# A hybrid diffusion trunk step on one core: the order of VectorE, ScalarE and TensorE around five waits of the trunk

## The reference, cut to what matters

```
h = rms_norm(x) * (1 + sc1) + sh1                    # sh1, sc1, ... = silu(cond) @ w_ada + b_ada
u2, q, k, v, f, g = split(h @ w_in)
conv = silu(layer_norm(depthwise_conv31(glu(u2)))) @ w_conv_out
attn = attention(q, k, v) @ w_na_out
fnet = fft2(f).real @ w_fnet
merged = g0 * conv + g1 * attn + g2 * fnet           # g = sigmoid(g)
x = x + gate * (merged @ w_out)                      # then the routed mixture of 16 experts
```

## Time and profile before

| what | value |
|---|---|
| time, median of 3 runs | 1264.2 us (1263.97 to 1264.5) |
| span of the profiled execution | 1264.8 us, 18871 instructions |
| TensorE busy | 1195.7 us, 95% of the span |
| VectorE busy | 907.1 us, 72% |
| ScalarE busy | 612.8 us, 48% |
| GpSimd busy | 298.6 us, 24% |
| moved | 301.32 MB, mean 238 GB/s |
| TensorE's share of the chain that ended last | 83% |

### The profile page before, as it was taken

One profiled execution on the slowest core, in us unless ns is written; L12 is line 12 of the kernel. 1 busy time (PEld: TensorE's weight loads), 2 busy tenths in 40 slices (PEclk: granted clock), 3 DMA queues, 4 the chain that ended last, 5 costly groups with the idle time before them and its releaser, 6 DMA issues.

```text
span 1264.8 us, 18871 instructions
## 1 busy us (share of the span) xinstructions
PE 1195.7 (95%) x7351; PEld 964.5 (76%) x7351; DVE 907.1 (72%) x1027; ACT 612.8 (48%) x688; POOL 298.6 (24%) x204
## 2 busy tenths in 40 slices
PE   4899999999998998999995999999999999999995
PEld 3788789989988998999994566666666666666663
DVE  2599656457765445227557699999999999999996
ACT  3421232234432223122223577777777777777774
POOL 1051001004432232323203022221112222222224
PEclk9899999999999998999996999999999999999998
DMA  9875528231111221254339999999999999999994
GB/s 322 284 203 177 184 68 200 68 103 41 67 34 38 72 67 59 69 182 151 103 117 335 363 382 380 385 389 381 381 381 380 379 379 380 381 381 381 381 327 177
DMA packets 156522, 301.32 MB, mean 238 GB/s; under 512 B 7059, under 2 KB 61335, under 8 KB 156466
## 3 DMA queue, kind: packets, MB, share of 16 engines
q1 hardware_dynamic: 145894, 271.23, 59.8%
q0 software_dynamic: 3872, 12.78, 4.6%
q10 hardware_dynamic: 6700, 16.51, 3.6%
HBM read 285.41 MB, written 15.08 MB: 238 GB/s over the span
## 4 chain that ended last, share of the span: by engine, by line
PE 83%; DVE 11%; ACT 2%; issue 2%; DMA 2%; POOL 1%; SPq 0%; ACTq 0%; POOLq 0%; DVEq 0%
PE bank L1598 17%; PE bank L1599 16%; PE bank L1600 16%; PE bank L1622 5%; PE bank L1624 4%; PE bank L1623 4%; PE bank L1627 4%; PE bank L1625 4%; PE bank L1626 4%; DVE fa L1122 4%; PE bank L1885 2%; DMA xg_f<-in_x_sample 1%; PE bank L1870 1%; PE bank L2112 1%; PE bank L1860 1%
## 5 line engine op out<-in xcount | busy, mean ns | idle before, releaser
L1598 PE MATMUL bank<-h2r_a,xTh 128*80 128x512 f32 x384 | 151.3, 394 | 1.2 <-DVE xTl L1514 1.2
L599 POOL TENSOR_TENSOR half<-half 1x1 f32<-1x1 f32 x33 | 67.8, 2053 | 349.0 <-DVE ye L1564 346.1
L1600 PE MATMUL bank<-h2r_a,xTl 128*80 128x512 f32 x384 | 149.5, 389 | 0.0
L959 ACT CAST h2r_a<-w_a 128x2048 fp32r<-128x2048 f32 x64 | 122.6, 1915 | 55.4 <-PE bank L1600 55.4
L528 POOL TENSOR_TENSOR lring<-wring,hring 128x2048 fp32r<-128x2048 f32 x20 | 95.7, 4786 | 164.8 <-ACT hring L670 164.8
L1599 PE MATMUL bank<-l2r_b,xTh 128*80 128x512 f32 x320 | 125.7, 393 | 0.0
L1508 DVE TENSOR_TENSOR l2r_b<-w_a,h2r_b 128x2048 fp32r<-128x2048 f32 x48 | 110.4, 2299 | 17.7 <-ACT h2r_b L959 17.7
L1122 DVE SCALAR_TENSOR_TENSOR fa<-fa,cwT 128x655 f32<-128x655 f32 x120 | 121.7, 1045 | 1.4
L1622 PE MATMUL bank<-hTh,hring 128*128 128x320 f32 x320 | 104.7, 327 | 4.2 <-DVE lring L1105 2.7
L959 ACT CAST h2r_b<-w_a 128x2048 fp32r<-128x2048 f32 x48 | 91.8, 1913 | 31.9 <-PE bank L1600 31.9
L1624 PE MATMUL bank<-hTl,hring 128*128 128x320 f32 x320 | 99.5, 311 | 0.0
(11 more groups left out here) (369 smaller groups left out, 3132.2 us busy)
## 6 DMA issues: line engine op xcount, KB each, us to landing
w_a<-in_w_e_up SPq DMA_DIRECT2D x64, 1024.0 KB, 14.3
w_b<-in_w_e_down SPq DMA_DIRECT2D x48, 1024.0 KB, 13.7
w_r<-in_w_e_gate SPq DMA_DIRECT2D x32, 1024.0 KB, 13.5
w_a<-in_w_e_gate SPq DMA_DIRECT2D x32, 1024.0 KB, 14.6
wring<-in_w_in SPq DMA_DIRECT2D x20, 1024.0 KB, 5.4
w_a<-in_w_e_down SPq DMA_DIRECT2D x16, 1024.0 KB, 14.1
fa<-in_w_ada SPq DMA_DIRECT2D x14, 1024.0 KB, 8.9
wring<-in_w_ada SPq DMA_DIRECT2D x10, 1024.0 KB, 10.8
```

Of the source, the lines that this page charges most:

```text
L959: act.copy(h2r[k % 3], w2[k]).then_inc(e_hi, 1)
L1598: pe.matmul(out, lh, rh, start=start, stop=False)
L1600: return pe.matmul(out, ll, rh, start=False, stop=stop)
```

## The change

- `f` stage, TensorE: the first `ada` and `ada_sum` of a block stand in the middle of the block, the second pair at its end. `ada_sum(23)` moves behind the first transform `uv(0)`.
- `f` stage, VectorE: the first `rows_out` and `ada_mod` of a block move ahead of the wait for ScalarE's copy of the block and the fold.
- Branches, TensorE: the first block waits for the low parts chunk by chunk (each chunk for its own count) in place of one wait for all four.
- `fnet`, VectorE: two taps, then the first `product`, two taps, the second `product`, and only then the rest of the taps.
- Layer norm, ScalarE: the read-outs of gate blocks g1(6) and g1(7) move ahead of and between the four `normed` steps; VectorE does two of the four final multiplications after the first two `na` products.

No operation is added or dropped; four waits take the place of one in each branch.

```diff
--- before.py
+++ after.py
@@ -904,12 +904,18 @@
                 act.copy(bh[:, c, 0:NP], Q[:, c, 0:NP])
                 act.copy(bh[:, c, NP:T].rearrange("p (r n i) -> p r n i", r=ROWS, n=4), by_block(Q[:, c, NP:T])).then_inc(s_bh, 1)
 
-            for c in range(CB):
+            def normed(c):
                 act.wait_ge(s_yr, c + 1)
                 act.activation(Yq[:, c, :], Yc[:, c, :], ACT.Tanh, bias=hlnb[:, 4 + c:5 + c], scale=hlnb[:, c:c + 1])
                 act.activation(Yc[:, c, :], Yc[:, c, :], ACT.Identity, bias=colsT[:, 16 + c:17 + c],
                                scale=colsT[:, 12 + c:13 + c]).then_inc(s_yt, 1)
-            gates("g1", "fnet", range(6, 8))
+
+            gates("g1", "fnet", range(6, 7))
+            normed(0)
+            normed(1)
+            gates("g1", "fnet", range(7, 8))
+            normed(2)
+            normed(3)
             u = U_OF[("na", 0)]
             act.wait_ge(s_job, J_OF[("na", 3)] + 1)
             hi(u + 2)
@@ -1217,14 +1223,14 @@
 
             for i in range(4):
                 n = J_OF[("f", i)]
+                rows_out(16 + 2 * i)
+                ada_mod(15 + 2 * i)
                 dve.wait_ge(s_fh, 2 * i + 1)
                 x, y, w = fs[:, i % 2, :], eo[:, i % 2, :], i % 2
                 dve.tensor_tensor(y[:, 1:HALF], x[:, 1:HALF], x[:, NS - 1:HALF:-1], ALU.add)
                 dve.tensor_tensor(y[:, HALF + 1:NS], x[:, 1:HALF], x[:, NS - 1:HALF:-1], ALU.subtract)
                 dve.tensor_copy(y[:, 0:NS:HALF], x[:, 0:NS:HALF]).then_inc(s_eo, 1)
                 dve.tensor_tensor(bl[:, i, 0:NP], bank_a(n)[:, 0:NP], bh[:, i, 0:NP].bitcast(F32), ALU.subtract).then_inc(s_jd, 1)
-                rows_out(16 + 2 * i)
-                ada_mod(15 + 2 * i)
                 rows_out(17 + 2 * i)
                 ada_mod(16 + 2 * i)
                 if i == 1:
@@ -1322,9 +1328,10 @@
                 ins.then_inc(s_jd, 1)
 
             split_lo(lambda c: Z[:, c, :], 0)
-            conv(CB * CW)
+            conv(2)
             for b in range(DC):
                 product("fnet", b)
+                conv(2 if b == 0 else CB * CW)
 
             dve.wait_ge(s_cv, CB * CW)
             for c in range(CB):
@@ -1358,14 +1365,19 @@
             for c in range(CB):
                 dve.tensor_tensor(Yc[:, c, NP:T], Yc[:, c, NP:T], bank[4][:, :], ALU.mult)
                 dve.tensor_tensor(Yc[:, c, 0:NP], Yc[:, c, 0:NP], bank[5][:, 0:P], ALU.mult).then_inc(s_yr, 1)
-            for c in range(CB):
+            def silu_of(c):
                 dve.wait_ge(s_yt, c + 1)
                 dve.scalar_tensor_tensor(Yc[:, c, :], Yq[:, c, :], 1.0, Yc[:, c, :], ALU.add, ALU.mult).then_inc(s_yz, 1)
+
+            silu_of(0)
+            silu_of(1)
             n0 = freed(J_OF[("fnet", 7)])[1]
             for b in range(DC):
                 product("na", b)
                 dve.wait_ge(s_jd, n0 + b + 1)
                 dve.tensor_tensor(M[:, b, :], M[:, b, :], G[:, b, :], ALU.add).then_inc(s_gm, 1)
+                if b < 2:
+                    silu_of(2 + b)
             dve.wait_ge(s_yz, CB)
             split_lo(lambda c: Yc[:, c, :], 2 * CB)
             n0 = freed(J_OF[("na", 7)])[1]
@@ -1608,7 +1620,7 @@
             def slot(u):
                 return unit_view(split(u)[0], u), unit_view(split(u)[1], u)
 
-            def block_steps(n, u, c0, xh, xl, nk, wait_h=False):
+            def block_steps(n, u, c0, xh, xl, nk, wait_h=False, low_before=None):
 
                 wh, wl = slot(u)
                 (t0, b0), (t1, b1) = job_halves(n)
@@ -1617,6 +1629,8 @@
                         bank_free(n)
                     if wait_h:
                         pe.wait_ge(s_h, c + 1)
+                    if low_before is not None:
+                        pe.wait_ge(s_bl, low_before + c + 1)
                     a_h, a_l = wh[:, c, c0:c0 + P], wl[:, c, c0:c0 + P]
                     st, en = c == 0, c == nk - 1
                     pe.matmul(b0, a_h, xh[:, c, t0], start=st, stop=False)
@@ -1730,11 +1744,12 @@
             for b in range(4):
                 steps, u = in_block("f", b)
                 lo_ready(pe, u)
-                run(steps)
                 for i in (16 + 2 * b, 17 + 2 * b):
+                    for _ in range(DC // 2):
+                        next(steps)
                     ada(i)
                     ada_sum(i - 1)
-            ada_sum(23)
+                run(steps)
 
             def uv(g):
 
@@ -1801,6 +1816,7 @@
 
             pe.wait_ge(s_cast, 4)
             uv(0)
+            ada_sum(23)
             v0 = v_unit(0)
             token_major("v", 0, 0, v0)
             uv(1)
@@ -1923,9 +1939,7 @@
                     u = U_OF[(kind, b // 4)]
                     if b % 4 == 0:
                         lo_ready(pe, u)
-                    if b == 0:
-                        pe.wait_ge(s_bl, n_split)
-                    run(block_steps(J_OF[(kind, b)], u, P * (b % 4), bh, bl, CB))
+                    run(block_steps(J_OF[(kind, b)], u, P * (b % 4), bh, bl, CB, low_before=n_split - CB if b == 0 else None))
 
             def gate(kind, b):
                 steps, u = in_block(kind, b)
```

## The result

| | before | after |
|---|---|---|
| median of the runs | 1264.19 us (1263.97 to 1264.5, 4 runs) | 1251.18 us (1249.95 to 1255.87, 4 runs) |
| ratio | | 0.9914, 95% from 0.9896 to 0.9932 |
| span of the profiled execution | 1264.8 us | 1250.5 us |
| TensorE busy | 1195.7 us | 1190.6 us |
| VectorE, ScalarE, GpSimd busy | 907.1, 612.8, 298.6 us | 907.9, 612.6, 297.4 us |

The ratio and its interval are those on record; the quotient of the two medians alone would be 0.9897. The kernel became faster, and the work is the same: VectorE, ScalarE and GpSimd are busy as long as before.

A forecast was written before the change was run, and what follows sets the result against it. TensorE, nearly always busy in the trunk, was taken as the bound. Savings of 0.5 + 2.2 + 1.9 + 3.8 + 4.4 = 12.8 us gave a 1252.0 span and 1251.4 median; 8-in-10 range 1248.8 to 1257.

The forecast's parts named there:

- `f` stage: f stage: mid-block groups start `uv` 1.06 us earlier; with `ada_sum(23)` behind `uv(0)`, 0.5 us is saved.
- low parts of `fnet`: Start of `fnet`: the first chunk no longer waits for all four low parts; 2.2 us saved.
- first product: Third `fnet` block: the product follows two taps and isn't held by GpSimd's pass, so TensorE's wait goes; 1.9 us.
- gate read-outs: Between the last g1 matmul and `na`: the read-out of g1(6) is hidden ahead of `normed`; 3.76 us saved.
- The stall: End of the f stage: TensorE's wait moves from the sums to the weight transfer of `ada(23)`; 1.7 us.
- The bound of 2.1: f stage: upper bound of the saving, if the weight unit for `ada(23)` lands in time; 2.1 us.
- The clock: `fnet` and `na`: the half-clock stretches go with the waits ahead of them; 1.6 and 2.8, together 4.4 us.
- B: Trunk: the waits go, but the clock falls once or twice all the same; 1253 to 1255.8 us, chance 0.20.
- A: Whole kernel: all comes as worked out; 1249.0 to 1253 us, chance 0.60.
- C: VectorE: one of its new orders is held by GpSimd's pass, 3.5 to 6 us given back; 1255 to 1257.5, chance 0.10.
- D: Behind the trunk: a transfer or the routing holds the experts, so nothing comes through; 1264 us, chance 0.05.
- E: f stage: mid-block groups thin out TensorE's work and the clock falls there; up to 1279.6 us, chance 0.05.

The follow-up runs named there:

- the first experiment: The kernel before with the f stage edits alone (mid-block groups, VectorE's rows ahead of the fold, `ada_sum(23)` behind `uv(0)`): 1262.59 us, ratio 0.9997.
- the second measurement: The changed kernel run once more, unaltered, beside the kernel before: 1252.36 us, ratio 0.9925.
- both additions together: The changed kernel with unit in 8 made one f block earlier and ScalarE's high part held until VectorE scaled the conv output: 1249.46 us, ratio 0.9895.

## Why the prediction was right, point by point

| term | predicted | measured |
|---|---|---|
| `f` stage, up to the first `uv` | 1.06 | 1.02 |
| the same, with `ada_sum(23)` behind `uv(0)`, up to `q` | 0.5 | 0.32 |
| low parts of `fnet`, from `q` to `fnet` | 2.2 | 2.22 |
| first product, with the fall behind it | 1.9 + 1.6 | 3.57 |
| gate read-outs | 3.76 | 3.76 |
| fall in `na` | 2.8 | 2.80 |
| sum, `f` to `conv` | 12.8 | 12.67 |
| ahead of `f` | 0 | 2.13 |
| behind `conv` | 0 | -0.46 |
| span | 12.8 | 14.3 |

**The f stage.** The step that counted was to ask what `ada(23)` waits for once the sums no longer wait. The stall was forecast at 1.7 and is 1.50 (1.67 with this part alone), and its cause is shown, since an earlier low part takes it away. The bound of 2.1 for a unit in time was nearly reached, 1.02 + 1.28 = 2.30 against 2.6 at the first `uv`. Up to `q` 0.32 came of 0.5, since `ada_sum(23)` behind `uv(0)` costs 0.70 and not 0.52 (`uv` to `q` 48.40, before 47.70). What remains of the term is smaller than the scatter of the stages behind it: in the kernel with this part alone the way from `f` to `fnet` is 267.27 us, 267.17 before.

**Low parts and first product.** Both are right in size, and shown to be no independent terms: alone the low parts give nothing, alone the product gives 1.9, and 3.58 with the fall that is missing in that profile. In the prediction they stand as 2.2 and 1.9 side by side, though its own due time for the product (386.2, against 391.75 before) used both. The product was indeed not held, and the tap behind it was.

**The gate read-outs.** As worked out, with GpSimd's pass coming earlier and VectorE's addition held (3.58, forecast "some 3"). The margin at the fourth block, forecast 0.9, is 0.8. Without the split multiplications it costs 5.64 us, more than the one pass, 4.8, that the prediction gave as the most: the wait of 2.58 is within it, the fall behind the wait was left out.

**The clock.** The size was that of the profile it was read from, 4.4, and the reason half right. "If the waits go, what preceded the fall goes" held: behind waits that are gone no profile here (the changed kernel twice, and the ones with its stalls taken away) has a fall in a branch. But the fall does not belong to the wait. The waits of 2.65 and 1.75 were followed by a fall in the kernel before and by none in two of the experiments; a wait of 2.42 had none and one of 2.58 had one. Only with `na`'s wait of 3.6 was there a fall in every profile that has it (four), of 6.8 us in three and 3.4 in one, and one behind the wait of 4.04 in the only profile with that. So it was right to give the falls a rival of their own (B). The Trainium skill ("TensorE: Matmul & The Clock Gate", Part 1) calls the moment of the change run-variable; it says so of the rise at a kernel's start, and these traces show the like of the falls.

This has a consequence for the sum. The 4.4 is what *this* execution of the kernel before lost, not what each loses, and that 12.67 came out so near to 12.8 is partly luck: the first experiment, with the same code in both branches as before, lost 2.75 less in them. The medians differ by 13.0 us, but the ratio, 0.9914, is 10.9 us with an interval from 8.6 to 13.1, and the second measurement, 0.9925, is 9.5. Both lie between the 8.4 without the clock and the 12.8 with all of it.

The mean granted clock, which the record has for every run, says more. In 47 runs of the kernel before it is 0.980 to 0.987, 0.9827 in the mean, and a lower clock goes with a longer time: of the 27 runs of the first series the three at 0.981 took 1264.35 us in the mean, the eight at 0.984 took 1260.05. In ten runs of the changed kernel it is 0.982 to 0.987, 0.9840 in the mean. One less the clock, times the time, gives as an estimate 21.8 us lost before and 20.0 after, so 1.8 of the 9.9 us between the mean times. It would be 3.5 if the longer half clock in routing (below), where TensorE has little to do, were left out. Either is less than 4.4. So executions of one kernel differ in what they lose to the clock; in which stage the runs without a profile lost it isn't shown, since this clock is a mean over the whole span.

**What was not foreseen.** The `u2` stage started 2.1 us earlier in the profiled execution, with no changed code ahead of it. The third group of `ada` starts at 24.97 before and at 24.98 after. The fourth group (L1654, now L1668), before and after:

```profile
30.02 1.94 PE L1654 MATMUL bank<-fa 128*32 128x256 f32 x16
28.56 1.07 PE L1668 MATMUL bank<-fa 128*32 128x256 f32 x16 [0.17 <-DMA fa<-in_w_ada]
```

The same 16 matmuls take 1.94 us in one and 1.07 in the other, so TensorE left its slow rate about one group later in the kernel before. Over the twelve profiles this makes two kinds: seven have the fourth group at 1.07 us and start `u2` at 37.15 to 37.48 us, five have it at 1.54 to 1.94 and start it at 39.14 to 39.82. The profile's clock column reads 1.00 in both there, so that this is the clock is argued from the durations, not shown. In routing the clock stayed at half for some 24 us instead of 20.5. Neither is in the sum, and each is smaller than the scatter of the runs (1249.95 to 1255.87), so that the forecast lies 0.2 from the median is closer than the reasoning can claim. The lower end of the stated range, 1248.8, has a slip: with the transfer in time the stage gains 2.1 and not 0.5, which makes 1251.4 - 1.6 = 1249.8. Nothing rests on it.

**The rivals.** A held. B did not occur in the changed kernel's two profiles, but it isn't excluded for its two slowest runs, 1255.87 and 1255.96 us, both at a mean clock of 0.982 and without a profile. C is real one tap, or one multiplication, away from the chosen order, at 2.66 and 5.64 us, against the 3.5 to 6 it was priced at. D and E are refuted: the last matmul comes earlier by all that the trunk saves, less 0.5, and the f stage with groups in mid-block has a clock of 1.00.

## What to carry to other kernels

Work out a stall by what is due next, not by its length: of three waits that were shortened here, one gave nothing without its neighbour, one uncovered a transfer of nearly the same length, and one was whole. When an engine's step is brought forward, follow what it triggers (here a GpSimd pass) and place what it would hold behind the work that is waited for; one tap of 0.8 us on the wrong side of that pass cost 2.7. A fall that is read in one profile belongs to that execution; a profile of a kernel with the same code in that stage shows whether it stays. And take the loss to a fallen clock as something that a wait makes possible in some executions: count it in the range, and compare stages from a common mark, not spans, when looking for an edit of a microsecond.

## What the hardware showed that was not expected

- The same two waits of TensorE, 2.65 and 1.75 us, nine microseconds apart, led to a granted clock of 0.50 for 3.4 us in one kernel and to 1.00 in two others whose code there is the same.
- A VectorE operation that GpSimd's pass holds ends behind the pass by nearly the time that it takes alone: 0.7 us for a tap of 0.81 (pass over at 388.11, the pair of taps at 389.62 with one tap behind the held one), 0.28 for a scaling of 0.48 (pass over at 415.15, scaling at 415.43).
- TensorE's first `ada` groups run at 1.94 us for 16 matmuls and later ones at 1.07. Where this changes differs from profile to profile by one group, and moves the start of the first long stage by some 2 us, as much as two of the five terms of this change. The granted clock reads 1.00 on both sides of it.
- In one of twelve profiles (both additions together) the `u2` stage has no half clock; with it, that stage ends 2 us sooner. No run here tells what decides it.
